# Sums of h moved from GpSimd to VectorE, a third weight sum written to another buffer, weight blocks loaded in another order, and weight quarters split at other places of a head step

## The reference

```python
for l in range(DEPTH):
    shift, scale, gate = ada_modulate(c, w_ada[l], b_ada[l])
    if l == N_A:
        ctx, kv_state = build_ctx(x)                  # shared k and v, compressed k and v
    h = rms_norm(x, g_norm[l]) * (1 + scale) + shift
    y = pool_mixer(h, ...) if l < N_A else nsa_mixer(h, ...)
    x = x + gate * y
return rms_norm(x, g_final), ...

# nsa_mixer
proj = h @ w_in                                       # q, three z (one per branch), 48 gate columns
o_cmp = softmax(q kc + bias) vc                       # compressed branch
o_slc, o_win = the same over selected and window keys
y = sum(gates * o * silu(z), over the three branches)
return y @ w_out
```

## Time and profile before

| | us |
|---|---|
| median of 3 runs (2493.14 to 2494.43) | 2494.03 |
| profiled execution, whole | 2493.92 |
| its span in the trace | 2492.1 |
| PE busy | 2392.4 (96%) |
| DVE busy | 1109.8 (45%) |
| ACT busy | 808.1 (32%) |
| POOL busy | 400.9 (16%) |

### The profile page before, as it was taken

How to read it: one execution, slowest core, us unless ns; L and a number is a source line. 1 busy time by engine, 2 the same in 40 slices (tenths; PEclk the granted TensorE clock), 3 DMA queues, 4 the chain that set the end, 5 groups by cost and what they waited for, 6 DMA issues and landing times.

```text
span 2492.1 us, 49177 instructions
## 1 busy us (share of the span) xinstructions
PE 2392.4 (96%) x20518; PEld 2248.3 (90%) x20518; DVE 1109.8 (45%) x1957; ACT 808.1 (32%) x1355; POOL 400.9 (16%) x508
## 2 busy tenths in 40 slices
PE   7999999999999999999889999999999999998997
PEld 6888888888899999999789999998888998867997
DVE  1236111221263353333867777555555455554433
ACT  1125111122232241111544444344444444432222
POOL 2002000790000000100410000122222222223000
PEclk9999999999999999999999999999999999998998
DMA  9985887676553356663444444433232323497232
GB/s 342 335 301 189 261 272 228 204 228 217 167 181 122 123 177 188 197 197 107 110 110 126 125 128 126 134 94 94 85 85 77 85 85 94 127 321 295 85 93 87
DMA packets 365378, 411.30 MB, mean 165 GB/s; under 512 B 21990, under 2 KB 321254, under 8 KB 362786
## 3 DMA queue, kind: packets, MB, share of 16 engines
q1 hardware_dynamic: 349538, 345.51, 44.5%
q0 software_dynamic: 15648, 62.97, 7.6%
HBM read 379.40 MB, written 51.08 MB: 173 GB/s over the span
## 4 chain that ended last, share of the span: by engine, by line
PE 79%; DVE 8%; ACT 5%; issue 5%; DMA 2%; SPq 0%; POOL 0%; DVEq 0%; ACTq 0%; POOLq 0%
PE acc L2414 52%; PE acc L2565 9%; PE work L2329 4%; PE work L2269 2%; DVE w_lo L1534 2%; PE out_acc L2653 2%; PE work L2617 1%; PE work L2690 1%; PE acc L2269 1%; PE work L2317 1%; ACT probs L1416 1%; DVE block_lo L1871 1%; PE work L2638 1%; DVE probs L1991 1%; DMA block<-in_w_in_b 1%
## 5 line engine op out<-in xcount | busy, mean ns | idle before, releaser
L2414 PE MATMUL acc<-h_hi,w_hi 128*128 128x260 f32 x3872 | 804.1, 289 | 26.1 <-DVE w_lo L1534 19.2
L2414 PE MATMUL acc<-h_hi,w_lo 128*128 128x260 f32 x3872 | 780.9, 283 | 0.0
L2414 PE MATMUL acc<-h_lo,w_hi 128*128 128x260 f32 x3872 | 780.0, 283 | 0.0
L2414 PEld LDWEIGHTS acc<-h_hi,w_hi 128*128 128x128 f32 x3872 | 597.1, 189 | 62.4 <-issue 39.2
L1534 DVE TENSOR_TENSOR w_lo<-raw,w_hi 128x1024 fp32r<-128x1024 f32 (+1 forms) x252 | 327.7, 1301 | 656.6 <-ACT w_hi L1113 656.4
L2414 PEld LDWEIGHTS acc<-h_lo,w_hi 128*128 128x128 f32 x3872 | 598.4, 189 | 0.0
L2414 PEld LDWEIGHTS acc<-h_hi,w_lo 128*128 128x128 f32 x3872 | 598.0, 189 | 0.0
L1113 ACT ACTIVATE w_hi<-raw 128x1024 fp32r<-128x1024 f32 (+1 forms) x252 | 265.2, 1053 | 802.4 <-PE acc L2414 789.4
L1871 DVE TENSOR_TENSOR block_lo<-block,block_hi 128x1024 fp32r<-128x1024 f32 x112 | 137.0, 1223 | 82.6 <-ACT block_hi L1354 82.6
L1354 ACT ACTIVATE block_hi<-block 128x1024 fp32r<-128x1024 f32 x112 | 118.3, 1057 | 135.9 <-DVE block L1906 43.7
L1047 POOL TENSOR_TENSOR probs<-probs,row_stats 128x128 f32<-128x128 f32 (+3 forms) x128 | 111.3, 898 | 274.8 <-DVE row_stats L2006 274.8
(11 more groups left out here) (392 smaller groups left out, 2825.9 us busy)
## 6 DMA issues: line engine op xcount, KB each, us to landing
ada<-in_w_ada SPq DMA_DIRECT2D x192, 512.0 KB, 4.8
raw<-in_w_in_a SPq DMA_DIRECT2D x64, 512.0 KB, 5.0
block<-in_w_in_b SPq DMA_DIRECT2D x64, 512.0 KB, 4.5
raw<-in_w_in_b SPq DMA_DIRECT2D x64, 512.0 KB, 4.0
raw<-in_w_kv SPq DMA_DIRECT2D x48, 512.0 KB, 3.7
raw<-in_w_out_a SPq DMA_DIRECT2D x32, 512.0 KB, 3.8
raw<-in_w_out_b SPq DMA_DIRECT2D x32, 512.0 KB, 3.5
pages_early<-in_cache_k_cmp SPq DMA_DIRECT2D x32, 256.0 KB, 4.4
```

The source lines that it names most:

```text
L2414: last = mm_(out[half][0:n, 0:HT], part[slot][:, kk, cols_], src[:, k, half * HT:(half + 1) * HT], start=(first and part is HI and src is ...
```

## The change

- The three sums of h that GpSimd made are now made by VectorE, each at a place of its own in VectorE's list: the second sum between the splits of gate quarters 1 and 2, the third between those of quarters 2 and 3, the last behind `sum_s2(0)`. GpSimd now writes the zeros of the padding instead, and ScalarE waits for that by GpSimd's semaphore.
- S3 is written over A11, and P7 is split from there. The loads follow: A11 and A21 of the first pair each start when their own gate quarter is split; in later pairs A21 comes first, behind S3, then A22, then A11 behind the split of P7.
- The first quarter of the heads waits for the split of the last P7 instead of the last S3.
- In the heads `MID` and `LATE` give way to separate tables for ScalarE and VectorE.

```diff
-PROD_ROLE = (R_A11, R_S, R_S, R_A22, R_A21, R_A12, R_A12)
+PROD_ROLE = (R_A11, R_S, R_S, R_A22, R_A11, R_A12, R_A12)
-MID = {0: (1,), 3: (5,)}
-LATE = {0: (2,), 1: (3,), 2: (4,), 3: (6,), 4: (7,), 5: (8,)}
+HI_FIRST = {0: (1,), 2: (4,), 3: (5,), 5: (8,)}
+HI_LAST = {0: (2,), 1: (3,), 3: (6,), 4: (7,)}
+LO_FIRST = {0: (1,), 2: (3,), 3: (5,), 5: (7,)}
+LO_NEXT = {2: (4,), 5: (8,)}
+LO_LAST = {0: (2,), 3: (6,)}
...
+            sp.wait_ge(lo_ready, 4 * Q_G + 1)
+            block_load(0, R_A11, 0, 0)
             for q in range(N_PAIR):
-                sp.wait_ge(lo_ready, 4 * Q_G + 1)
+                if q == 0:
+                    sp.wait_ge(lo_ready, 4 * Q_G + 2)
                 wait(sp, s_sum, 4 * (q - 1) + 3)
-                block_load(q, R_A11, 0, 0)
+                block_load(q, R_A21, 0, P)
...
                 block_load(q, R_A22, 8, P)
-                sp.wait_ge(lo_ready, P_0 + N_PROD * (q - 1) + S_P7 + 1)
-                block_load(q, R_A21, 0, P)
+                if q:
+                    sp.wait_ge(lo_ready, P_0 + N_PROD * (q - 1) + S_P7 + 1)
+                    block_load(q, R_A11, 0, 0)
...
-                        sp.wait_ge(s_sum, 4 * N_PAIR - 1)
+                        sp.wait_ge(lo_ready, P_0 + N_PROD * (N_PAIR - 1) + S_P7 + 1)
...
-            nc.gpsimd.tensor_tensor(t3, b22, t3, ALU.subtract).then_inc(t_sums, 1)
-            nc.gpsimd.tensor_tensor(b22, b22, t1, ALU.subtract).then_inc(t_sums, 1)
-            nc.gpsimd.tensor_tensor(b21, b22, b21, ALU.subtract).then_inc(t_sums, 1)
+            for j in range(4):
+                last = nc.gpsimd.memset(RAW[j][:, :, 48:P], 0.0)
+            last.then_inc(s_cz, 1)
...
-            act.wait_ge(dve_set, SET_PAD)
+            act.wait_ge(s_cz, 3)
...
                     elif u in (2, 5):
                         z_out(i, u // 3, 0)
-                        quarters(LATE[u])
                         z_out(i, u // 3, 1)
...
-                V.tensor_tensor(RB[R_A21][:, :, :], RB[R_A11][:, :, :], RB[R_A21][:, :, :], ALU.subtract).then_inc(s_sum, 1)
+                V.tensor_tensor(RB[R_A11][:, :, :], RB[R_A11][:, :, :], RB[R_A21][:, :, :], ALU.subtract).then_inc(s_sum, 1)
...
-                    quarters((u + 1,) if last_turn else MID.get(u, ()))
+                    quarters((u + 1,) if last_turn else LO_FIRST.get(u, ()))
                     softmax(i, u)
+                    if not last_turn:
+                        quarters(LO_NEXT.get(u, ()))
                     if not first or u >= 2:
                         weighed(i, u)
                     factor(i, u)
                     if not last_turn:
-                        quarters(LATE[u])
+                        quarters(LO_LAST.get(u, ()))
```

More of the change, by code:

```diff
@@ L188, in slot_of @@
     return (p + 2) % 3
-MID = {0: (1,), 3: (5,)}
-LATE = {0: (2,), 1: (3,), 2: (4,), 3: (6,), 4: (7,), 5: (8,)}
+HI_FIRST = {0: (1,), 2: (4,), 3: (5,), 5: (8,)}
[3 more added lines that the diff above has]
+LO_LAST = {0: (2,), 3: (6,)}
 FIRST_HALF = (0, 3, 5, 8, 11, 13, 16)
 N_TURN = 8
-SET_NEG, SET_PAD, SET_GATES, SET_HEADS = 1, 2, 3, 4
+SET_NEG, SET_GATES, SET_HEADS = 1, 2, 3
 def ahead(q):
@@ L735, in pair_store @@
                 sp.dma_start(pair_scr[q % 2][q // 2][:, TP * c:TP * c + TP], STG[c][:, 0:TP]).then_inc(st_out[c], 16)
+            sp.wait_ge(lo_ready, 4 * Q_G + 1)
+            block_load(0, R_A11, 0, 0)
             for q in range(N_PAIR):
-                sp.wait_ge(lo_ready, 4 * Q_G + 1)
+                if q == 0:
+                    sp.wait_ge(lo_ready, 4 * Q_G + 2)
                 wait(sp, s_sum, 4 * (q - 1) + 3)
-                block_load(q, R_A11, 0, 0)
+                block_load(q, R_A21, 0, P)
                 if q == 0:
                     sp.wait_ge(lo_ready, 4 * Q_G + 3)
-                sp.wait_ge(lo_ready, P_0 + N_PROD * (q - 1) + S_P4 + 1)
+                else:
+                    sp.wait_ge(lo_ready, P_0 + N_PROD * (q - 1) + S_P4 + 1)
                 block_load(q, R_A22, 8, P)
-                sp.wait_ge(lo_ready, P_0 + N_PROD * (q - 1) + S_P7 + 1)
-                block_load(q, R_A21, 0, P)
+                if q:
+                    sp.wait_ge(lo_ready, P_0 + N_PROD * (q - 1) + S_P7 + 1)
+                    block_load(q, R_A11, 0, 0)
                 if q == 0:
                     sp.wait_ge(lo_ready, 4 * Q_G + 4)
-                sp.wait_ge(lo_ready, P_0 + N_PROD * (q - 1) + S_P3 + 1)
+                else:
+                    sp.wait_ge(lo_ready, P_0 + N_PROD * (q - 1) + S_P3 + 1)
                 block_load(q, R_A12, 8, 0)
@@ L965, in _ @@
             apply(1)
-            pool.wait_ge(t_sums, 1)
-            pool.wait_ge(h_ready, 3 * KT)
-            b21, b22 = X[:, 8:KT, 0:HT], X[:, 8:KT, HT:T]
-            t1, t3 = X[:, 0:8, 0:HT], X[:, 0:8, HT:T]
-            nc.gpsimd.tensor_tensor(t3, b22, t3, ALU.subtract).then_inc(t_sums, 1)
-            pool.wait_ge(t_sums, 2)
-            nc.gpsimd.tensor_tensor(b22, b22, t1, ALU.subtract).then_inc(t_sums, 1)
-            pool.wait_ge(t_sums, 3)
-            nc.gpsimd.tensor_tensor(b21, b22, b21, ALU.subtract).then_inc(t_sums, 1)
+            pool.wait_ge(cw1, 17)
+            for j in range(4):
+                last = nc.gpsimd.memset(RAW[j][:, :, 48:P], 0.0)
+            last.then_inc(s_cz, 1)
             pool.wait_ge(cout, 18)
@@ L1458, in heads @@
                         turned(i, u)
-                    quarters((u + 1,) if last_turn else MID.get(u, ()))
+                    quarters((u + 1,) if last_turn else HI_FIRST.get(u, ()))
                     exps(i, u)
@@ L1466, in heads @@
                         z_out(i, u // 3, 0)
-                        quarters(LATE[u])
                         z_out(i, u // 3, 1)
                     else:
-                        quarters(LATE[u])
+                        quarters(HI_LAST[u])
                 if last_turn:
@@ L1857, in _ @@
             apply(1)
-            dve.wait_ge(cw1, 17)
-            for j in range(4):
-                last = V.memset(RAW[j][:, :, 48:P], 0.0)
-            last.then_inc(dve_set, 1)
             compress_out(16)
@@ L1927, in block_out @@
                     V.tensor_tensor(STG[0][:, HT:T], D[1][:, 0:HT], U2[:, :], ALU.add).then_inc(st_added, 1)
+            dve.wait_ge(h_ready, 3 * KT)
+            b21, b22 = X[:, 8:KT, 0:HT], X[:, 8:KT, HT:T]
+            t1, t3 = X[:, 0:8, 0:HT], X[:, 0:8, HT:T]
+            V.tensor_tensor(t3, b22, t3, ALU.subtract).then_inc(t_sums, 1)
             lo(Q_G, 2)
+            dve.wait_ge(t_sums, 2)
+            V.tensor_tensor(b22, b22, t1, ALU.subtract).then_inc(t_sums, 1)
             lo(Q_G, 3)
@@ L1935, in _ @@
             sum_s2(0)
+            dve.wait_ge(t_sums, 3)
+            V.tensor_tensor(b21, b22, b21, ALU.subtract).then_inc(t_sums, 1)
             t_lo(1)
@@ L2081, in _ @@
             dve.wait_ge(s_bd, 16 * 2)
-            dve.wait_ge(s_cz, 3)
+            dve.wait_ge(s_cz, 4)
             def rows_out(n):
```

## The result

| | before | changed |
|---|---|---|
| median, us | 2493.7 (2493.14 to 2494.43, 4 runs) | 2463.06 (2459.47 to 2463.45, 4 runs) |
| profiled execution / its span | 2493.92 / 2492.1 | 2462.76 / 2461.1 |
| POOL busy | 400.9 | 376.2 |

The ratio is 0.9874, 95% interval 0.9857 to 0.9891: faster by 31 us. The time lies inside the range and 1.4 us under the forecast of 2464.5. As will be seen, this closeness is partly luck: one term was too large, and another that was too small and the scatter of the clock made up for it.

The account below looks back on a forecast made before the run. TensorE is busy 2392 of 2492 us, so only its idle time and slow clock can go. Gates 9 and heads 20.4 make 29.4 us off 2493.9, giving 2464.5; range 2458 to 2477.

Parts of the forecast that it names:

- Gate quarters: Gates and first pair: with the sums on VectorE, TensorE's waits for low parts go; 6.4 us gained up to P7.
- the sums don't explain the splits: Rival, gates: low parts stay at 3.4 us without GpSimd's sums beside them, so nothing is gained there; 2478 us, chance 0.05.
- Second pair: Wait of 4.22 us before the second pair's P1: loading A21 and A22 first, A11 last, gains 3 us.
- The 9: Term for the gates' stage and the second pair's P1 together: 9 us, between 6 and 12.
- Heads: Moved weight-quarter splits save 1.14, 1.83 and 0.18 us in each of 6 turns and 1.46 in the first: 20.4 us.
- The rival that the 1.83 comes back in unit 3's scores: Heads, unit 3: the scores wait for what the half no longer waits for; 12.4 us lost, 2477 us, chance 0.12.
- The rival with quarter 7: Heads: quarter 7's split, now amid GpSimd's products, comes late; 0.9 us in each of 6 turns, 2470 us, chance 0.07.
- A11 late in every pair: Rival, 15 pairs: A11 lands too late for P1, costing landing time less 6.05 us each, up to 97 us; chance 0.06.
- the last turn and the stages behind it: End of the heads and everything after: forecast as unchanged.

Follow-up runs that it names:

- pool_reads: The changed kernel plus twelve GpSimd additions that read SBUF, beside the splits of the gates' weight quarters; 2470.35 us in its one run.
- start_only: The changed kernel with the weight quarters of the heads at their old places; 2487.03 us, ratio to before 0.9972.
- q48_only: The changed kernel with quarters 3 and 7 split by VectorE at their old places, 4 and 8 still early; 2468.34 us, ratio to before 0.9896.
- q37_only: The changed kernel with quarters 4 and 8 at their old places on ScalarE and VectorE, 3 and 7 still moved; 2484.09 us, ratio to before 0.9963.
- changed_again: The changed kernel run once more, unaltered, for comparison on the same chip as later kernels; 2463.32 us, ratio to before 0.9866.

## Why the prediction was right, and where it was wrong

**Gate quarters: right to 0.3 us.** Forecast: low parts of 0.65, quarters and P1 without a gap from 1221.9 to 1237.8, gates at 1240.2, P7 at 1253.0. Measured: 0.69, 1221.7 to 1237.9, 1240.1, 1253.3. The third sum does lie in VectorE's chain, from 1238.78. There is some luck in the start: the stage began 0.8 later in this profile, and the eight small products ahead of the quarters took 1.08 us instead of 1.88, at the higher clock level. The Trainium skill's rule (SBUF — State Buffer, section "SBUF: two separate sides") held in each point that was tried: an operation with two SBUF inputs against one of GpSimd that reads, held for one instruction (a split of 5.12 us that ends 0.55 after the sum), memsets free (690 ns). The rival "the sums don't explain the splits" falls with these 690 ns and with `pool_reads`.

**Second pair: the mechanism wrong, 3 us forecast.** The step that failed is "I take 3, nearer to the good end, since the two loads that S1 needs go out together", and with it "A11, which is needed three products later". A11 is needed at once: VectorE's list has the split for P1 behind S1 and three short instructions. So P1 waits for whichever of the three loads lands third, A21 before and A11 now, and a new order among them can give only the 1.3 us named above. All three are late because of the twelve small stores that go out just ahead of them on GpSimd's queue: the third landed in 11.6 us before and in 12.0 now. The stores moved forward by 6.6 us, and the loads by 6.2. I had read the 90% busy engines at 130 GB/s without asking who shared them.

The stall itself was 4.82 us where it was 4.22, for TensorE came to it earlier. P1 of the second pair still stands 7.1 earlier (1273.99 and 1266.92), and 1.1 of that is lost behind it, where TensorE was at the lower clock level for twice as long as before. The stage gave 5.9 up to the heads, or 6.7 counted from its own start, against 9. In four other profiles with the same code there (`start_only`, `q48_only`, `q37_only`, `changed_again`) it gave 7.6 to 10.0 from its own start. The 9 lies within this scatter, but the reason that I gave for it is not what happens.

**Heads: the steps right, the size too small.** 20.4 forecast, 23.5 measured, of which the turns give 6 times 3.6 and the first 1.9. In unit 2 it was 1.06 (I had 1.14). In unit 3 it was 2.01 where I had 1.83, in unit 5 to the next turn 0.53 where I had 0.18, in the first turn 1.64 where I had 1.46. The printed wait is counted from the end of the last matmul's record. In a steady run a matmul of 0.28 us is followed by the next after 0.12, so TensorE could have gone on 0.16 earlier than the record ends. A wait that disappears gives its printed length and 0.16 more; 1.83 and 1.46 then come out as 1.99 and 1.62. A wait that only shrinks, as in unit 2, gives the difference. About 0.2 in each turn, in unit 5, stays unexplained.

**What is late next.** The rival that the 1.83 comes back in unit 3's scores (0.12) did not happen: no such wait is printed, and the segment gained 2.01. The rival with quarter 7 (0.07) did not either. The split now lies in the midst of GpSimd's products, and takes 1.29 instead of 1.23. The last row is the last of the four products:

```profile
1710.63 1.29 DVE L1538 TENSOR_TENSOR w_lo<-raw,w_hi 128x1024 fp32r<-128x1024 f32 x1
1709.09 3.73 POOL L1052 TENSOR_TENSOR probs<-probs,row_stats 128x128 f32<-128x128 f32 x4 [9.60 <-DVE row_stats L2014]
1710.80 2.02 POOL L1052 TENSOR_TENSOR probs<-probs,row_stats 128x512 f32<-128x512 f32 x1
```

The split began as the third product was ending, and then it was GpSimd that waited: its last product took 2.02 us instead of the 1.04 before.

**A11 late in every pair** (0.06) did not happen: no pair after the second waited for a load in the changed kernel. That such landings occur was right, but in the changed kernel all four loads that took over 7 us lie behind the twelve stores.

**The rest.** I had the last turn and the stages behind it unchanged. They gave 1.6: the last turn lost 1.5 to a stretch at the lower clock, and the tail had some 7 us less at that level, which is 3 won. No part of the change explains either, and I count it as the scatter of the clock between executions.

The sum: 5.9 + 23.5 + 1.6 = 31.0. The forecast had 9 + 20.4 + 0 = 29.4. The first term came out 3.1 smaller and the second 3.1 larger, so that only the 1.6 of the clock is left between the two sums: that is luck.

## What to carry to other kernels

Look for an operation that takes several times what its size says, and see what the neighbour engine does in that time: moving GpSimd's three sums onto the busier engine, at 7 us of its time, was a gain. Value a wait that disappears by the pace of the starts, not only by its printed length; a printed wait of 0.44 us, repeated 14 times, was worth 10 us and one moved line. When a load is slow, list the transfers of all queues ahead of it before reordering its own queue, and ask which of the loads lands last and who waits for it.

## What the runs showed of the hardware

- VectorE's operations with two SBUF inputs, beside GpSimd instructions that read SBUF, ended about their own time after the end of the GpSimd instruction at work: splits of 0.69 us took up to 5.12 beside sums of 5 us and 1.7 beside additions. A copy with one input from an accumulator (0.67) and all operations beside memsets were not longer. GpSimd waits in the same way: an addition of 1.28 us took 3.29 beside a VectorE sum.
- Twelve transfers of 32 elements of 4 bytes, 1.5 KB in all, made three block loads of 512 KB land in 10 to 14 us instead of 4.6, at each of three places.
- A wait of TensorE of 1.8 us was followed by a stretch at 1.2 GHz in four of six inner turns of one kernel, in one of six of another and in none of a third with the same wait; with it the wait cost 1.5 us more.
